# Expert outputs added onto a stored residual by DMA instead of being gathered and summed in the closing stage

## What is computed

```python
f = hierarchical_moe(x, ...)             # 32 experts, each token goes to 2 of them
x = layer_norm(ALPHA * x + f, ln_g[i, 1], ln_b[i, 1])

# inside hierarchical_moe, after the routing:
xs = xf[tok_s]                            # rows sorted by expert
h = silu(ragged_dot(xs, w1, sizes)) * ragged_dot(xs, w3, sizes)
o = ragged_dot(h, w2, sizes) * gate_s[:, None]
y = zeros_like(xf).at[tok_s].add(o)       # each token sums its two gated rows
```

## Time and profile before

| what | us |
|---|---|
| median of 3 runs | 5849.02 (5843.36 to 5855.09) |
| the profiled execution, its own time | 5865.35 |
| its span in the profile | 5863.7 |
| expert stage of layer a, first `up` product to last `outputs` copy | 2520.5 to 3393.6 |
| expert stage of layer b, the same | 4891.5 to 5753.4 |
| closing stage of layer a, first to last `sn` instruction | 3398.0 to about 3504 |
| closing stage of layer b, first `sn` instruction to the end of the span | 5757.8 to 5863.7 |

### The profile page before, as it was taken

How to read it: one execution, slowest core, us unless ns; L and a number is a source line. 1 busy time by engine, 2 the same in 40 slices (tenths; PEclk the granted TensorE clock), 3 DMA queues, 4 the chain that set the end, 5 groups by cost and what they waited for, 6 DMA issues and landing times. The chain is left out here.

```text
span 5863.7 us, 110758 instructions
## 1 busy us (share of the span) xinstructions
PE 5373.1 (92%) x36410; PEld 4504.7 (77%) x36411; DVE 3828.9 (65%) x6597; ACT 2846.8 (49%) x4819; POOL 1281.2 (22%) x957
## 2 busy tenths in 40 slices
PE   7999999999898979789999968998999887999997
PEld 5889788898788867678787836978888676788773
DVE  5678887778555558675866556775444555755795
ACT  3343444444477766355665404343777114645671
POOL 2010020000000000054655331100000003544583
PEclk9999999999999989889999988999999897999998
DMA  5776777667799986477988565654453425866987
GB/s 168 208 193 206 202 220 210 178 187 196 222 316 311 318 274 192 153 254 258 332 297 298 205 270 168 196 165 143 149 160 117 139 90 206 311 247 244 343 308 283
DMA packets 888320, 1310.04 MB, mean 223 GB/s; under 512 B 186014, under 2 KB 547149, under 8 KB 887948
## 3 DMA queue, kind: packets, MB, share of 16 engines
q1 hardware_dynamic: 756060, 939.81, 51.0%
q0 software_dynamic: 77168, 294.67, 14.7%
q10 hardware_dynamic: 54720, 70.60, 3.6%
HBM read 974.87 MB, written 348.87 MB: 226 GB/s over the span
## 5 line engine op out<-in xcount | busy, mean ns | idle before, releaser
L520 PE MATMUL qa_ps_out<-qa_x_hi,qa_w_hi 128*128 128x512 f32 x1344 | 535.2, 398 | 44.4 <-DVE qa_w_lo L644 27.6
L520 PE MATMUL qa_ps_out<-qa_x_hi,qa_w_lo 128*128 128x512 f32 x1344 | 530.0, 394 | 0.0
L520 PE MATMUL qa_ps_out<-qa_x_lo,qa_w_hi 128*128 128x512 f32 x1344 | 529.9, 394 | 0.0
L557 ACT ACTIVATE qa_w_hi<-qa_w_whole 128x1024 fp32r<-128x1024 f32 x180 | 191.3, 1063 | 456.4 <-DVE qa_w_whole L635 287.7
L520 PE MATMUL qa_ps_out<-qa_w_hi,qa_x_hi 128*128 128x256 f32 x1344 | 382.7, 285 | 7.2 <-DVE qa_w_lo L644 7.2
L520 PE MATMUL qa_ps_out<-qa_w_hi,qa_x_lo 128*128 128x256 f32 x1344 | 381.4, 284 | 0.0
L520 PE MATMUL qa_ps_out<-qa_w_lo,qa_x_hi 128*128 128x256 f32 x1344 | 381.3, 284 | 0.0
L1996 POOL TENSOR_TENSOR b_ex_w_lo<-b_ex_w_raw,b_ex_w_hi 128x1024 fp32r<-128x1024 f32 x128 | 351.3, 2780 | 129.7 <-ACT b_ex_w_hi L1993 129.7
L1996 POOL TENSOR_TENSOR a_ex_w_lo<-a_ex_w_raw,a_ex_w_hi 128x1024 fp32r<-128x1024 f32 x128 | 348.0, 2750 | 138.4 <-ACT a_ex_w_hi L1993 133.6
L2494 DVE CUSTOM_DVE_ANT_0 ga_minus_s<-ga_ps_s,ga_bias 128x512 f32<-128x512 f32 (+1 forms) x256 | 194.1, 758 | 258.2 <-PE ga_ps_s L2433 189.0
L1085 ACT ACTIVATE da_prob<-da_minus_s,da_rows 128x256 f32<-128x256 f32 (+1 forms) x768 | 317.7, 464 | 46.6 <-DVE da_rows L1053 45.2
(11 more groups left out here) (442 smaller groups left out, 15589.7 us busy)
## 6 DMA issues: line engine op xcount, KB each, us to landing
a_ex_w_raw<-w SPq DMA_DIRECT2D x128, 1024.0 KB
b_ex_w_raw<-w SPq DMA_DIRECT2D x128, 1024.0 KB
qa_w_raw<-w_qkv_a SPq DMA_DIRECT2D x144, 512.0 KB
a_ex_w_raw<-w POOLq DMA_DIRECT2D x66, 1024.0 KB
b_ex_w_raw<-w POOLq DMA_DIRECT2D x66, 1024.0 KB
da_q_cross<-qT SPq DMA_DIRECT2D x48, 1024.0 KB
da_k_parts<-kT SPq DMA_DIRECT2D x48, 1024.0 KB
ys<-qa_x_rows POOLq DMA_DIRECT2D x64, 512.0 KB, 4.2
```

Source lines behind the costliest of these rows:

```text
L520: done = pe.matmul(out, stationary, moving, start=(k == 0 and i == 0), stop=(k == KH - 1 and i == 2))
L557: act.activation(w_hi[:, p % W_RING], src, ACT.Copy).then_inc(w_hi_done, 1)
```

## The change

The experts' rows are scaled by their gates as they leave PSUM and added to the residual in DRAM by the DMA itself.

- `merge_and_norm` stores x1 a second time, into a new DRAM tensor `sums`. Both tensors get 128 rows more than there are tokens. The extra rows of x1 are zeroed by one DMA in `project_qkv`, where the 64 DMAs over `ys` are gone; those of `sums` are zeroed at the start of each expert stage, from `y`, which POOL clears first.
- `route_tokens` makes `at_block` twice, once with the token and once with the gate in the marked place (one more 128 x 2048 VectorE step), so the 32 products have 128 columns instead of 64. From the second half it makes `shares`, the gate of each row divided by ALPHA. Empty places now point to the extra rows. After the products VectorE has six small steps in place of two.
- In `experts` VectorE multiplies by the row's share instead of copying, after a copy of one column (`share`). SyncE no longer stores. POOL starts its body with `add_y_two_before`: wait for `y` of block b-2, copy the column of tokens, issue an indirect DMA that adds the 128 rows of `y` to rows of `sums`.
- `sum_and_norm` reads one row per token from `sums` (its norm is that of the old sum, since both are scaled by ALPHA and the epsilon is divided by ALPHA squared). PE has nothing left to do. VectorE measures and makes the inverse root and its product with minus the mean, ScalarE centres and scales (L2284 of the new kernel), POOL multiplies by the gain (L2269), VectorE adds the shift two tiles later (L2323). SyncE loads and stores.

```diff
 def route_tokens(...)
-                tt(at_block[:], iota[:, 0:B].unsqueeze(1).unsqueeze(1).to_broadcast([P, T, TOP_K, B]),
+                tt(at_block[:, :, :, 0], iota[:, 0:B].unsqueeze(1).unsqueeze(1).to_broadcast([P, T, TOP_K, B]),
                    block_of[:].unsqueeze(3).to_broadcast([P, T, TOP_K, B]), ALU.is_equal)
+                tt(at_block[:, :, :, 1], at_block[:, :, :, 0],
+                   gates[:].unsqueeze(3).to_broadcast([P, T, TOP_K, B]), ALU.mult)
...
                 dve.wait_ge(inverted, 1)
-                link(dve.memset(routing.tokens[:, B:B + 1], 0))
-                link(dve.tensor_copy(routing.tokens[:, 0:B], ps_tokens[:]))
+                link(dve.tensor_copy(place[:, 0:B], ps_tokens[:, 0]))
+                link(dve.tensor_scalar(empty[:], place[:], 0.0, None, ALU.is_equal))
+                link(dve.scalar_tensor_tensor(out=place[:], in0=empty[:], scalar=own_row[:], in1=place[:], op0=ALU.mult,
+                                              op1=ALU.add))
+                link(dve.tensor_scalar(place[:], place[:], float(TOKENS), None, ALU.add))
+                link(dve.tensor_copy(routing.tokens[:], place[:]))
+                link(dve.tensor_scalar(routing.shares[:], ps_tokens[:, 1], 1.0 / ALPHA, None, ALU.mult))
 def merge_and_norm(...)
                     act.dma_start(scratch.x1[bass.ts(t, P), :], x1[:, t % 2, :]).then_inc(x1_stored[t % 2], 16)
+                    act.dma_start(scratch.sums[bass.ts(t, P), :], x1[:, t % 2, :]).then_inc(x1_stored[t % 2], 16)
 def experts(...)
                 def body(b, at):
-                    store_y(b - 2)
                     next_w13(b, at.count)
...
                 def outputs(b):
+                    dve.wait_ge(y_done, 2 * b + 2)
+                    dve.tensor_copy(share[:], routing.shares[:, bass.ds(b, 1)]).then_inc(shared, 1)
+                    dve.wait_ge(shared, b + 1)
                     dve.wait_ge(y_stored, 16 * b + 16)
                     dve.wait_ge(w2_used, W2_PIECES * b + 2 * W2_PIECES)
                     for h in range(2):
-                        dve.tensor_copy(y[:, bass.ts(h, HALF)], ps_y[:, h, :]).then_inc(y_done, 1)
+                        dve.tensor_scalar(y[:, bass.ts(h, HALF)], ps_y[:, h, :], share[:], None, ALU.mult
+                                          ).then_inc(y_done, 1)
...
+                def add_y_two_before(b):
+                    pool.wait_ge(y_done, 2 * b)
+                    pool.tensor_copy(y_column[:], routing.tokens[:, bass.ds(b - 2, 1)]).then_inc(y_picked, 1)
+                    pool.wait_ge(y_picked, b)
+                    pool.sem_inc(stepped, 1)
+                    pool.indirect_dma_start(out=scratch.sums, out_offset=bass.IndirectOffsetOnAxis(
+                        ap=y_column[:, 0:1], axis=0), in_=y[:], in_offset=None, compute_op=ALU.add
+                    ).then_inc(y_stored, 16)
...
                 def body(b, at):
+                    add_y_two_before(b)
+                    rest(b, at)
...
+                pool.memset(y[:], 0.0).then_inc(y_cleared, 1)
                 gather_x(0)
```

231 lines of the change are left out of this document (110 added, 121 removed).

## The result

The changed kernel took 5884.94 us (median of 5 runs, 5879.93 to 5889.09), the kernel before, run beside it, 5852.01. The ratio is 1.0051 with a 95% interval from 1.0035 to 1.0067: **slower by about 30 us**, clear of what a measurement can tell, and outside the range of the prediction. The profiled execution of the changed kernel spans 5885.1 us, 21 more than that of the kernel before.

| stage | before, a / b | after, a / b | change, both layers | predicted |
|---|---|---|---|---|
| merging | 284.9 / 271.0 | 285.9 / 272.1 | +2.1 | 0 |
| routing | 49.8 / 49.8 | 51.6 / 51.4 | +3.4 | +7.2 |
| experts, end of routing to last y | 885.9 / 874.2 | 914.5 / 905.5 | **+60** | +10 |
| last y to first closing instruction | 4.4 / 4.4 | 13.4 / 13.2 | **+17.8** | +6 |
| closing, with its store | 107.6 / 105.9 | 84.5 / 84.1 | **-45** | -30 |

The account below looks back on a forecast made before the run. PE was taken to bound the expert stage, and the PE chain the closing stage. Terms: 2 x (-15 + 3 + 3.6 + 5) - 0.5 = -7.3 us, so 5849 - 7 = 5842, range 5804 to 5878.

Parts of the forecast that it names:

- What bounds the kernel: Expert stage: PE busy 839.31 of 860 us, so edits on other engines count only where PE waits for them.
- the lock: VectorE steps with two SBUF inputs and POOL steps exclude each other: 1219 and 2418 ns alone, longest 3433 and 3417.
- Closing stages: Closing stage: gathers and PE products go, tile period becomes 4.75 us, 91 us against 105.9, so -15 per layer.
- small steps slip past the lock: Rival, closing stages: VectorE's 3.8 us a tile bounds, -30 each instead of -15, total 5812; chance 0.20.
- End of the experts: Last y to next stage: POOL's copy, step and issue plus the DMA's read, add and write, +3 per layer (1.6 to 6).
- Routing: Routing stage: one more 128 x 2048 step, 2.29, and small steps, +1.3; products unchanged; +3.6 per layer.
- Expert loops: Expert blocks: POOL's added work costs +37, fewer collisions give -27; net +5 per layer, bounds -20 to +54 for both.
- starting POOL's low parts later moves them off VectorE's: Expert loops: four collisions of 6.8 us each avoided, -27.
- The other +37 of that term: Expert loops: 17 of 91 used blocks with under 1.2 us of slack lose about 2.2 us each.
- The slower rival: POOL's queue becomes the bound in runs of new experts: +54 instead of +10 in the loops, total 5886; chance 0.14.
- The DMA share: Expert stage: the adding DMA moves 0.5 MB more per block, raising 0.77 to at most 0.85, still no bound.

Follow-up runs that it names:

- the one-input steps: Changed kernel with three small VectorE steps of the closing stage (check, rstd, back) taking one tensor input, other values as scalar operands: 5872.58 us, ratio 1.0024.
- The self-waits: Changed kernel where each of POOL's low parts of w3 after the first waits for the one before to be complete: 5848.62 us, ratio 0.9985.
- the overwriting scatter: Changed kernel with an indirect DMA that overwrites the 128 rows instead of adding to them: 5842.52 us, ratio 0.9968.
- the spare gather: Kernel before with one more indirect gather per block, into an unread tile, at the head of POOL's loop: 5864.03 us, ratio 1.0005.

## Why the prediction was wrong

**What bounds the kernel**, and the lock between VectorE and POOL, were read rightly, and every large term came from them. The sum failed in the loops.

- **Closing stages, -15 per layer forecast, -22 measured.** The mechanism was right: the period is the chain that I wrote down, small steps, ScalarE's pass, POOL's whole product. Its size was off, 4.75 forecast, 4.29 measured. From the product's end to that of the small steps it is 0.6 us where I had 0.9, since the check stands ready and ends with the product; ScalarE's pass with its gaps takes 1.4 instead of 1.3, the product 2.34 instead of 2.42; and the guess, for which I added a part, lies beside ScalarE's pass. That is 6 of the 7 us, and the ends of the stage were 1 us shorter. The rival "small steps slip past the lock" was wrong as a fact, since the check was held, but its 3.8 us is what the one-input steps reached, with another bound: POOL's guess and product. On the Trainium skill's rule (GPSIMD Engine Reference, section 1, Specifications: contention with VectorE instructions that have two SBUF inputs) the runs agree down to one column: 956 ns with two inputs, 266 with one.
- **End of the experts, +3 forecast, +8.9 measured.** The steps that I counted (copy, 0.8, issue, a later landing) are there and make some 3 us; the rest of what POOL's being last costs has no row in the profile of before, where POOL had been idle for 21 us at that point. I gave bounds of 1.6 to 6 for a situation that no row showed.
- **Routing, +3.6 forecast, +1.7 measured.** The extra step and the small steps cost what was counted, but the products took 9.31 instead of 13.9, with a granted clock of 0.72 in place of 0.50, so the 2.24 us of waiting disappeared.
- **Expert loops, +10 forecast, +60 measured; this is the step that failed.** I wrote "starting POOL's low parts later moves them off VectorE's" and took 27 us off for it. The later start did the opposite. While the engines took turns, five blocks lost 5.4 to 7.0 us (6.8 in the earlier trace rows) and eight 1.3 to 2.6; directly behind the adding DMA they didn't take turns, and 12 blocks lost about 8 us each. The order of the queues showed that the adding DMA would stand directly ahead of the low parts; the trace of before had no case of a DMA instruction running straight into them, since w2 loads and a wait for ScalarE lay between (0.96 us of idle time at the least). I had the issue at 1.16 us by the gather's row; the adding one takes a median of 2.1 and 2.0. And of the 6.8 us about half is not waiting but the lower granted clock behind it (0.86 over that block). The self-waits, which put pauses between POOL's steps and leave the add in its place, gave back 39 us, more than the 33 by which the changed kernel is slower. The other +37 of that term, POOL's time in tight blocks, showed up when the long instructions were taken away: extra 56 to 73 us in place of 41, so 15 to 32 us.
- **The slower rival** had the size (+54 in the loops) and the place (runs of new experts), but named the gather as what comes late. The waits for `x_row` hardly grew; `gate` was late. That its total, 5886, lies next to the 5885 measured is chance: the closing stages gained 15 us more than it had, and the ends of the experts cost 12 more.
- **Not in the sum at all:** 0.07 us a block from the place of xT in SBUF, 6 to 7 us.
- **The DMA share** went from 0.77 to 0.85 over 2520 to 3380, as forecast, and was no bound. The bytes counted there did not grow (279 and 274 GB/s); with the overwriting scatter, at 277 GB/s, the share is 0.79.

## What to carry to other kernels

When work is added to an engine that has to take turns with another, ask not only how long it takes but what it now runs into without a pause: a short wait between wide steps (here 0.2 us each) can be worth more than it costs. In small steps beside a busy POOL, pass values as scalar operands, so that one tensor input is left. And count the end of a stage by which engine leaves last: POOL with an indirect DMA cost 6 to 9 us more there than SyncE with a plain store. And a stall of PE can cost more than its idle time: here 5 us of idle time brought 3 us of products at a lower clock.

## What the runs showed of the hardware

- VectorE and POOL, both with two inputs in SBUF, normally take turns (3.4 us for a pair of 1.2 and 2.4). A row of POOL steps directly behind an adding DMA instruction shut one VectorE instruction out for 11.1 us, in 12 blocks; behind a plain gather it was 6.3 to 9.7 us in seven blocks, behind an overwriting scatter never. A pause of 0.2 us between POOL's steps restored the turns.
- A VectorE step on one column with two SBUF tensors is held until the end of POOL's wide step (0.9 and 2.05 us instead of 0.21); with one tensor and scalar operands it isn't (0.27).
- The adding DMA of 128 rows takes POOL a median of 2.0 us to issue and lands after 7.4 us (layer b), the overwriting one 1.2 and 5.5; the gather of x1's rows takes 1.0 to issue, the spare gather at the add's place 1.2.
- Tiles 8 bytes further in SBUF lengthened a block's 72 products and 12 transposes by 0.07 us in all: with 4, 12 and 16 bytes of single columns ahead of xT the usual block took 18.10, 18.17 and 18.09 us, and with 8 bytes and a spare tile of 4 KB 18.12 to 18.13.
- After 5 us of idle time PE's products in the expert loop ran at the lower clock for a while: 0.87 granted over the block, 1.00 in a usual one.
